# Order of loads and splits in modulation; cumulative sums in exact parts and another order of products in linear attention

## The reference, cut to what matters

```python
m = jax.nn.silu(cond) @ w + b              # adaln_params: 1024 -> 3072, two conditions
shift, scale, gate = jnp.split(m, 3, axis=-1)
h = rms_norm(x, g) * (1 + scale) + shift   # 1024 rows of x, 256 of the context
```

```python
b = jnp.cumsum(la, axis=3)                 # la: log of the decays, <= 0
b_last = b[:, :, :, -1:, :]
d_state = einsum('bhncd,bhnce->bhnde', k * jnp.exp(b_last - b), v)
S = decay[..., None] * S + d_state         # scan over chunks
qd = q * jnp.exp(b);  kd = k * jnp.exp(-b)
att = jnp.where(tri, einsum('bhncd,bhnsd->bhncs', qd, kd), 0.0)
o = einsum('bhncs,bhnse->bhnce', att, v) + einsum('bhncd,bhnde->bhnce', qd, s_prev)
```

## Time and profile before

| | us |
|---|---|
| three runs | 3400.26, 3412.86, 3414.64 |
| median | 3412.86 |
| the profiled execution | 3402.91 |
| its span | 3401.0 |

### The profile page before, as it was taken

The page is one execution under the profiler, slowest core; times in us unless marked ns, Lnnn a source line. Parts: engine busy times, 40 slices in busy tenths (PEclk is TensorE's granted clock), DMA queues, the critical chain, the costliest instruction groups (busy, mean ns, idle before and its releaser), DMA issues. The chain is left out here.

```text
span 3401.0 us, 51118 instructions
## 1 busy us (share of the span) xinstructions
PE 3161.1 (93%) x20794; PEld 2786.1 (82%) x20794; DVE 1703.9 (50%) x2688; ACT 1215.3 (36%) x2256; POOL 321.7 (9%) x365
## 2 busy tenths in 40 slices
PE   7999979999898999899998988879988999999998
PEld 3999967777688999777788976768867999998877
DVE  3459826666572122265536316745644555544343
ACT  4313336666662343134434204544423111111232
POOL 1000011100010000132210110003300000000010
PEclk9999999999998999999999999989999999999999
DMA  5557560001233221243211435110012111112332
GB/s 188 163 172 238 173 229 26 26 14 69 81 149 111 80 78 61 102 167 114 93 49 33 117 96 122 39 20 9 21 64 81 43 49 43 44 49 80 99 130 93
DMA packets 203630, 307.24 MB, mean 90 GB/s; under 512 B 44136, under 2 KB 140200, under 8 KB 201388
## 3 DMA queue, kind: packets, MB, share of 16 engines
q1 hardware_dynamic: 183264, 232.05, 21.7%
q0 software_dynamic: 20176, 72.53, 6.5%
HBM read 228.76 MB, written 75.76 MB: 90 GB/s over the span
## 5 line engine op out<-in xcount | busy, mean ns | idle before, releaser
L115 PE MATMUL p_pb<-p_w_hi,h_hi 128*128 128x416 f32 (+2 forms) x1168 | 408.0, 349 | 6.8 <-PEq L69 5.3
L117 PE MATMUL p_pb<-p_w_hi,h_lo 128*128 128x416 f32 (+2 forms) x1168 | 405.7, 347 | 0.0
L116 PE MATMUL p_pb<-p_w_lo,h_hi 128*128 128x416 f32 (+2 forms) x1168 | 403.7, 346 | 0.0
L115 PEld LDWEIGHTS p_pb<-p_w_hi,h_hi 128*128 128x128 f32 x1168 | 221.2, 189 | 8.9 <-issue 5.6
L116 PEld LDWEIGHTS p_pb<-p_w_lo,h_hi 128*128 128x128 f32 x1168 | 220.8, 189 | 2.3
L117 PEld LDWEIGHTS p_pb<-p_w_hi,h_lo 128*128 128x128 f32 x1168 | 220.5, 189 | 0.7
L115 PE MATMUL fu_pf<-h_hi,up_first_hi 128*128 128x344 f32 (+1 forms) x528 | 169.7, 321 | 3.7 <-DVE fu_pf L3923 3.7
L117 PE MATMUL fu_pf<-h_hi,up_first_lo 128*128 128x344 f32 (+1 forms) x528 | 169.9, 322 | 0.0
L116 PE MATMUL fu_pf<-h_lo,up_first_hi 128*128 128x344 f32 (+1 forms) x528 | 169.7, 321 | 0.0
L116 PE MATMUL fu_pf<-h_lo,fu_w_hi 128*128 128x344 f32 (+1 forms) x528 | 169.7, 321 | 0.0
L115 PE MATMUL fu_pf<-h_hi,fu_w_hi 128*128 128x344 f32 (+1 forms) x528 | 169.1, 320 | 0.0
(11 more groups left out here) (589 smaller groups left out, 7515.4 us busy)
## 6 DMA issues: line engine op xcount, KB each, us to landing
up_raw<-in_ffn_up SPq DMA_DIRECT2D x88, 256.0 KB, 3.1
fd_raw<-in_ffn_down SPq DMA_DIRECT2D x44, 512.0 KB, 3.5
p_slab<-in_adaln_w SPq DMA_DIRECT2D x64, 256.0 KB, 3.3
la_qkv<-p SPq DMA_DIRECT2D x16, 1024.0 KB, 5.0
p<-p_o SPq DMA_DIRECT2D x60, 208.0 KB, 2.1
s_raw<-in_w_in POOLq DMA_DIRECT2D x48, 256.0 KB, 3.5
rT<-p_stage SPq DMA_DIRECT2D x10, 896.0 KB
p_raw<-in_ab_w_in POOLq DMA_DIRECT2D x10, 832.0 KB, 7.1
```

What stands on the lines that cost most here:

```text
L115: pe.matmul(out, left[0], right[0], start=start, stop=False)
L116: pe.matmul(out, left[0], right[1], start=False, stop=False)
L117: return pe.matmul(out, left[1], right[0], start=False, stop=stop)
```

## The change

In modulation block 0 comes in two loads, and PE starts on the first; each half of `raw` is issued behind block 2 and block 3; POOL issues two tiles of x after block 1 and the rest after block 3. The first weights are split between the norms of tiles 1, 2 and 3, each half as it lands; norms then run four tiles ahead, tile 0's high and low parts come directly behind its affine, and tile 0 is turned ahead of block 3's product.

In linear attention the decays' logs are split like weights: ACT writes the high part and POOL (for the first two units DVE) the low part, two units ahead; the matrix of the sums, whose values (0 and 1/16) are exact, is written as fp32r, and each sum is two fp32r matmuls. The state's product comes before the outer products and opens the accumulation, the values' product comes last and closes it; DVE adds a unit's output before it updates the state. All eight rows of the output weights are loaded at once at unit 2 into one buffer, which is the low part's own place.

```diff
-                    sp.dma_start(w[b % RING][:, :, :], w_v[:, :, 0, b, :]).then_inc(w_in[b % RING], 16)
-                for h in range(2):
-                    sp.dma_start(raw[h][:, :, :], first_w[:, half * h:half * h + half, :]).then_inc(ahead_in, 16)
+                    if b == 0:
+                        sp.dma_start(w[0][:, 0:half, :], w_v[:, 0:half, 0, b, :]).then_inc(front_in, 16)
+                        sp.dma_start(w[0][:, half:KD, :], w_v[:, half:KD, 0, b, :]).then_inc(w_in[0], 16)
+                    else:
+                        sp.dma_start(w[b % RING][:, :, :], w_v[:, :, 0, b, :]).then_inc(w_in[b % RING], 16)
+                    if b >= NB - 2:
+                        h = b - NB + 2
+                        sp.dma_start(raw[h][:, :, :], first_w[:, half * h:half * h + half, :]).then_inc(raw_in[h], 16)
...
-                for t in range(4):
+                for t in range(2):
                     load_x(t)
                 pool.wait_ge(w_in[1], 32)
-                for t in range(4, N):
+                for t in range(2, N):
...
-                for t in range(4):
-                    normalize(t)
+                normalize(0)
+                normalize(1)
+                weights_high(0)
+                normalize(2)
+                weights_high(1)
+                normalize(3)
...
                 for t in range(N):
-                    if t >= 2 and t + 2 < N:
-                        normalize(t + 2)
                     affine(t)
-                    if t:
-                        high(t - 1)
-                    if t == 1:
-                        weights_high()
+                    if t != 1:
+                        high(max(t - 1, 0))
+                    if t + 4 < N:
+                        normalize(t + 4)
...
+                weights_low(0)
+                finish(2)
                 spread(2)
-                spread(3)
-                finish(2)
+                weights_low(1)
                 finish(3)
...
                 for t in range(N):
-                    if t >= 2 and t + 2 < N:
-                        spread(t + 2)
                     affine(t)
-                    if t:
-                        low(t - 1)
-                    if t == 1:
-                        weights_low()
+                    if t == 0:
+                        spread(3)
+                    if t != 1:
+                        low(max(t - 1, 0))
+                    if t + 4 < N:
+                        spread(t + 4)
...
                 def step(t):
-                    if t == 0:
-                        pe.wait_ge(w_lo_done, 2)
                     pe.wait_ge(lo_done, t + 1)
                     if t >= 4:
                         pe.wait_ge(step_copied, t - 3)
                     for k in range(KD):
+                        if t == 0 and k % half == 0:
+                            pe.wait_ge(w_lo_done, k // half + 1)
...
                 for b in range(NB):
-                    pe.wait_ge(w_in[b % RING], (b // RING) * 16 + 16)
+                    if b == 0:
+                        pe.wait_ge(front_in, 16)
+                    else:
+                        pe.wait_ge(w_in[b % RING], (b // RING) * 16 + 16)
                     for k in range(KD):
+                        if b == 0 and k == half:
+                            pe.wait_ge(w_in[0], 16)
                         mm = pe.matmul(pm[b][0:2, :], g.act_c[:, k, :], w[b % RING][:, k, :], start=(k == 0), stop=(k == KD - 1))
                     mm.then_inc(made, 1)
-                for t in range(2):
-                    turn(t)
+                    if b >= NB - 2:
+                        turn(b - NB + 2)
...
-        sums_of = ph.sb("sums_of", [P, 2, 2, P])
+        sums_of = ph.sb("sums_of", [P, 2, 2, P], F32R)
+        la_parts = [ph.sb(name, [P, 2, GK], F32R) for name in ("la_hi", "la_lo")]
...
-                    if HI_AT <= n < HI_AT + KD:
-                        k = n - HI_AT
-                        if k >= 2:
-                            sp.wait_ge(w_lo, k - 1)
-                        sp.dma_start(op.raw[k % 2][:, :], w_v[:, k, :]).then_inc(raw_in[k % 2], 16)
+                    if n == HI_AT - 4:
+                        for k in range(KD):
+                            sp.dma_start(op.raw_rows[:, k, :], w_v[:, k, :]).then_inc(rows_in, 16)
...
+                    if n + 2 < NU:
+                        pool.wait_ge(la_hi, n + 3)
+                        lo_part(pool, la_parts[1][:, n % 2, :], la_of(n + 2), la_parts[0][:, n % 2, :]).then_inc(la_lo, 1)
                     if HI_AT <= n < HI_AT + KD:
                         k = n - HI_AT
                         pool.wait_ge(w_hi, k + 1)
-                        lo_part(pool, op.w[1][:, k, :], op.raw[k % 2][:, :], op.w[0][:, k, :]).then_inc(w_lo, 1)
+                        lo_part(pool, op.w[1][:, k, :], op.raw_rows[:, k, :], op.w[0][:, k, :]).then_inc(w_lo, 1)
...
+                def high(n):
+                    act.activation(la_parts[0][:, n % 2, :], la_of(n), ACT.Copy).then_inc(la_hi, 1)
+
+                high(0)
+                high(1)
...
+                    if n + 2 < NU:
+                        high(n + 2)
                     if HI_AT <= n < HI_AT + KD:
                         k = n - HI_AT
-                        act.wait_ge(raw_in[k % 2], 16 * (k // 2) + 16)
-                        act.activation(op.w[0][:, k, :], op.raw[k % 2][:, :], ACT.Copy).then_inc(w_hi, 1)
+                        act.wait_ge(rows_in, 16 * KD)
+                        act.activation(op.w[0][:, k, :], op.raw_rows[:, k, :], ACT.Copy).then_inc(w_hi, 1)
...
-                    ins = act.activation(op.raw[0][:, op.width * h:op.width * h + op.width], op.head(O0, h), ACT.Square, accum_out=op.ss[:, h:h + 1])
+                    ins = act.activation(la[:, NT, op.width * h:op.width * h + op.width], op.head(O0, h), ACT.Square, accum_out=op.ss[:, h:h + 1])
...
+                def first_low(n):
+                    dve.wait_ge(la_hi, n + 1)
+                    lo_part(dve, la_parts[1][:, n, :], la_of(n), la_parts[0][:, n, :]).then_inc(la_lo_first, 1)
...
+                first_low(0)
                 both = dec[:, :, :].rearrange("p t (h c) -> p t h c", c=2)
                 dve.wait_ge(zeroed, 1)
                 for d in range(2):
                     ch.step(dve.tensor_copy(since[:, :, d, :, 1 - d], both[:, 0:NT, G_HEADS * d:G_HEADS * d + G_HEADS, d]))
                 ch.link(dve.tensor_tensor(decays[:, :, :], both[:, :, :, 0], both[:, :, :, 1], ALU.mult))
                 dve.sem_inc(prepared, 1)
+                first_low(1)
...
+                    dve.wait_ge(values, u + 1)
...
-                    update(n)
                     if is_x(n):
                         add(n)
+                    update(n)
...
-                    la_d = la[:, tile, GK * d:GK * d + GK]
+                    hi, lo = (part[:, n % 2, :] for part in la_parts)
+                    if n < 2:
+                        pe.wait_ge(la_lo_first, n + 1)
+                    else:
+                        pe.wait_ge(la_lo, n - 1)
                     if is_x(n):
-                        pe.matmul(p_cum[:, :], sums_of[:, d, 0, :], la_d, start=True, stop=True).then_inc(cum, 1)
+                        pe.matmul(p_cum[:, :], sums_of[:, d, 0, :], hi, start=True, stop=False)
+                        pe.matmul(p_cum[:, :], sums_of[:, d, 0, :], lo, start=False, stop=True).then_inc(cum, 1)
                     if 1 <= n <= NX:
                         pe.wait_ge(exp_c, n)
-                    pe.matmul(p_rest[:, :], sums_of[:, d, 1, :], la_d, start=True, stop=True).then_inc(rest, 1)
+                    pe.matmul(p_rest[:, :], sums_of[:, d, 1, :], hi, start=True, stop=False)
+                    pe.matmul(p_rest[:, :], sums_of[:, d, 1, :], lo, start=False, stop=True).then_inc(rest, 1)
...
                     pe.wait_ge(masked, u + 1)
-                    if u:
-                        pe.wait_ge(added, u)
                     for h in range(G_HEADS):
-                        mm = pe.matmul(po[:, h, :], at[d][:, h, :], v(d, h), start=(h % 2 == 0), stop=False, skip_group_check=True)
+                        mm = pe.matmul(po[:, h, :], at[d][:, h, :], v(d, h), start=False, stop=True, skip_group_check=True)
                     mm.then_inc(values, 1)
 
                 def from_state(n):
                     d = units[n][0]
                     pe.wait_ge(upd, n - 1)
+                    if n > NX:
+                        pe.wait_ge(added, n - NX)
                     for h in range(G_HEADS):
-                        mm = pe.matmul(po[:, h, :], qtT[d][:, h, :], S[d][:, h, :], start=False, stop=True, skip_group_check=True)
+                        mm = pe.matmul(po[:, h, :], qtT[d][:, h, :], S[d][:, h, :], start=(h % 2 == 0), stop=False, skip_group_check=True)
                     mm.then_inc(state, 1)
 
                 warm_up(pe, g, po[:, 0, :], 10)
@@ -2333,13 +2372,13 @@
                         attend(n)
```

(33 more changed lines are left out.)

## The result

The kernel before took 3407.98 us (median of 20 runs, 3398.97 to 3418.33), the changed kernel 3421.24 us (20 runs, 3405.57 to 3434.96). The ratio is 1.0035, with a 95% interval of 1.0022 to 1.0048: some 13 us slower, inside the 0.5% that I had called no change, where the forecast of 3409 came out within 1 us of before. The profiled execution of the changed kernel took 3427.12 us around a span of 3425.3; that of before had a span of 3401.0.

A forecast was written before the change was run, and what follows sets the result against it. The prediction took modulation to wait for loads, then splits, and linear attention to be bound by PE's own list. From 3402.91 us, -10.3 and +11.5 gave 3404.1; 5 added for the runs' median made 3409, range 3391 to 3423.

The forecast's parts named there:

- Modulation: Modulation stage: earlier loads, earlier splits and a shorter end gain 10.3 us in all, between 7 and 12.
- 5.4 + 2.0: Modulation behind the first affine: splits moved ahead gain 5.4 us up to the second product, the stage's end 2.0.
- The tail's 2.0 us: End of modulation: only affine, high and low parts are left, no norm in between, gaining 2.0 us.
- The loop: Linear attention's steady units: the q, k, v load waits for the moved values' product, so a unit lasts 9.2 us.
- The order term: Linear attention's changed product order: 14 units of 9.22 us instead of 8.99 cost 3.3 us.
- Start and end: Linear attention: output weights' rows queued ahead of units 3 and 4 cost 3.7 us at the start; the end gains 1.0.
- The shared port: Linear attention: kl on POOL starting first delays qd on DVE by 1.1 us in five of 14 units, +5.5 us.
- Rival (b): Linear attention: kl is ahead of qd in every unit, costing 15.4 us instead of 5.5; 3414 (3419) us, chance 0.22.
- Rival (d): Linear attention: sums in parts are no cheaper, kl comes later and blocks less; -3 us, 3400 (3405), chance 0.05.
- The sum: Whole kernel: modulation's -10.3 and linear attention's +11.5 give +1.2 us.
- a frame of its own: Whole kernel: 5 us added to 3404.1, half the 10 by which the runs' median exceeds the profiled execution, giving 3409.

The follow-up runs named there:

- split: Changed kernel with q and k loaded apart from v, only v waiting for the values' product; ratio to before 0.9914, linear attention 168.4 us.
- port: Changed kernel with kl on POOL waiting until kd and qd of its unit are done; ratio to before 0.9986, linear attention 182.0 us.
- warm: Changed kernel with five dummy products on PE ahead of kd's transposes in each steady unit; ratio to before 1.0026, linear attention 192.0 us.

## Why the prediction was wrong, point by point

| stage, us | before, mean of four | changed, mean of four | difference | predicted |
|---|---|---|---|---|
| modulation, to the end of its last low part | 101.3 | 91.3 | -10.0 | -10.3 |
| from there to linear attention | 1298.8 | 1300.8 | +2.0 | 0 |
| linear attention | 177.3 | 192.7 | +15.4 | +11.5 |
| rest | 1827.3 | 1833.3 | +6.0 | 0 |
| span | 3404.6 | 3418.1 | +13.4 | +1.2 |

- **Modulation** was right in its sum: the last low part ended at 89.5 to 92.9, near 90 as written, and 10.0 us were gained in the mean, 7.5 in the profile on which the sum was built. Some of that is luck, as the parts erred both ways. Up to the first affine the mean of four gains 4.7 us, not 2.9, and behind it 5.3, not 5.4 + 2.0. In the first profile the first affine came at 48.44 (48.2 forecast) and the second product at 60.11 (59). Block 0 began 4.2 us earlier, not 1.5, but blocks 0 and 1 then took 16.38 us, so that they ended 3.5 us sooner, in the bounds given. Block 2 began at 28.25 (28.5, though 3.2 MB at 382 GB/s from 18.5 make 26.9: 1.6 us of the forecast aren't in its terms). x tile 2 was there at 40.03, not 41.0, so the last bias sum wasn't late, but block 3 ended at 45.9 and not 45.0. The tail's 2.0 us were 0.3 with all that lies behind the second product (7.2 us gained there, 7.5 at the end of the first profile): the last tiles follow each other by 3.8 us in both kernels, as a tile's affine waits for a low part, not for a norm.
- **The loop.** kd was released by DMA in all 14 units, the sums take 1.0 us, PE's own list is 8.2 us (split), and the 39 steady units of four profiles that weren't blocked last 9.22 us in the mean: all four as written. The order term, +3.3, stands.
- **Start and end.** Unit 5's scores began 43.3 us after the stage's start, not 39.5: +3.7, as written. The end gave 1.05 back, for 1.0. The Trainium skill (DMA: Bandwidth & Descriptors, Queues, rings and completion order) has descriptors of one queue consumed in ring order: the trace agrees, units 3 and 4 landed 11.9 and 11.2 us after their issue behind the rows, where the steady loads take 5.0.
- **The shared port is the step that failed, by its size.** It took five blocked units of 14 at 1.1 us each, 5.5 us, and priced only the delay of qd: what PE does after standing 2.1 us was put at nothing. There were 17 blocked units in four profiles, 4.25 an execution. The seven of them without a slow product last 10.5 us, 1.3 over the 9.22, so that four and a quarter of them make the 5.5 us of the forecast. The other ten, in which the clock fell, last 12.2 us, 1.7 more. Ten in four profiles are 4.1 us an execution, and linear attention was 15.4 us longer for the 11.5 forecast. Without a blocked unit (port) the stage is 182.0 us and not 192.7; with PE kept busy (warm) the slow products are gone.
- **Rival (b)** gives nearly the number that was measured (3419), and isn't what happened: three to six units were blocked, not all. **Rival (d)** pointed the right way, for the reason given there: with sums that are no cheaper, kl comes later. With the old sums the stage is 6.3 us longer than before, which modulation's gain of 10.0 turns into -3.7, near the -3 of the rival. I hadn't seen that it speaks against making the sums cheaper at all in this order, where they cost 6 to 12 us.
- **The sum.** The net of +1.2 was the difference of two terms of 10 and 11.5; over four profiles it is +13.4, 12 more. Of these 12 the port's clock is 4. The other 8 lie in stages outside the sum: 2 between the two changed ones, and 6 behind them, of which 5.4 are the stretch of the delta rule, long in three of the changed kernel's four profiles and in one of before's. The sum put them at nothing, the runs don't show their cause, and part of them may be chance. The forecast of 3409 was also set in a frame of its own: 5 us added to the profile's, where the median shown was 3412.86. Against that it said 4 us faster, against its own terms; over 20 runs before has its median at 3408, so that 3409 meant no change. That the result is still under the 0.5% called no change owes as much to the width of that bound as to the terms.

## What to carry to other kernels

When a product is moved, look at what waits for its end, a load's buffer first: a load that waits for a consumer of only half its data should be split. Here that was worth 24 us, where the changed stage had lost 15. A step that is made cheaper off the bound shifts whoever waits for it, and may bring it into the way of what is on the bound. And a delay that leaves PE standing for 2 us should be priced with a product at the lower clock behind it: here 1.7 us, in 10 cases of 17.

## What the hardware showed unexpectedly

- PE's granted clock fell after waits of 2.04 to 2.6 us between stretches at full clock, in 10 of 17 cases; the values' product behind them took 2.68 to 3.56 us against 1.89. With the wait at 1.1 us it fell in none of five (warm). What decides between the ten and the seven is open.
- One stretch of 3166 matmuls in the delta rule takes 184 to 186 or 192 to 197 us, at a granted clock near 0.96 or 0.90, in the same kernel.
- When kl starts ahead of qd, qd takes 1.75 us and kl 1.36; when it starts 0.3 us behind, qd takes 0.68 and kl 1.51 (alone 1.27). In the 56 steady units of the changed kernel's four profiles qd took 1.75 to 1.78 us in each of the 17 in which kl had started first, by 0.03 to 0.56 us, and 0.68 or 0.69 in each of the 39 in which it had not. (In warm one kl came first by 0.02 us and blocked nothing.) The Trainium skill has this rule (SBUF — State Buffer, Who interferes with whom): the order of issue decides who blocks; the trace agrees.
